# Rotary turns in a two-model kernel: halves exchanged by DMA in place of rotation products

## The reference

```python
def apply_rope(x, cos, sin):
    half = x.shape[-1] // 2
    xf = x.astype(jnp.float32)
    x1, x2 = xf[..., :half], xf[..., half:]
    return jnp.concatenate([x1 * cos - x2 * sin, x1 * sin + x2 * cos], axis=-1).astype(x.dtype)

qg = apply_rope(rms_norm(u_q.reshape(b, l, GQA_HEADS, HEAD_DIM), g_q_gqa), cos_g, sin_g)   # "a": 6 heads of 64, 2 key heads
qm = jnp.concatenate([qm[..., :64], apply_rope(qm[..., 64:], cos_m, sin_m)], axis=-1)      # "a": 6 MLA heads, last 32 of 96
q = rope(rmsnorm(two_map_heads(aq), q_norm_g), cos, sin)                                   # "b": 8 heads of 2 x 64, keys alike
```

## Time and profile before

| | us |
|---|---|
| median of 3 runs | 1923.73 (1923.69 to 1924.51) |
| profiled execution | 1922.46 |
| its span, first to last instruction | 1920.7 |
| PE busy | 1812.9 (94%) |
| DVE busy | 1103.0 (57%) |
| ACT busy | 886.3 (46%) |
| POOL busy | 378.6 (20%) |

### The profile page before, as it was taken

How to read it: one execution, slowest core, us unless ns; L and a number is a source line. 1 busy time by engine, 2 the same in 40 slices (tenths; PEclk the granted TensorE clock), 3 DMA queues, 4 the chain that set the end, 5 groups by cost and what they waited for, 6 DMA issues and landing times.

```text
span 1920.7 us, 28654 instructions
## 1 busy us (share of the span) xinstructions
PE 1812.9 (94%) x10864; PEld 1468.4 (76%) x10864; DVE 1103.0 (57%) x1955; ACT 886.3 (46%) x1773; POOL 378.6 (20%) x802
## 2 busy tenths in 40 slices
PE   4999999899999998988999989999999899999998
PEld 2453454588888885647999989888999797888998
DVE  3327841687777533482555567566556585664555
ACT  2227620433333333472555566565554464664542
POOL 1015100000000000240000025065451061364430
PEclk8799989999999999999899989999999999999999
DMA  8321631254555431302344533532344334332351
GB/s 303 104 86 54 216 126 44 88 175 176 176 175 187 163 88 40 117 1 78 142 176 176 176 132 105 187 116 101 135 160 176 128 104 176 132 132 88 133 177 65
DMA packets 139875, 255.26 MB, mean 133 GB/s; under 512 B 14926, under 2 KB 21724, under 8 KB 139612
## 3 DMA queue, kind: packets, MB, share of 16 engines
q1 hardware_dynamic: 138742, 251.16, 37.6%
q0 software_dynamic: 704, 2.10, 0.3%
q10 hardware_dynamic: 294, 0.18, 0.0%
HBM read 252.38 MB, written 1.05 MB: 132 GB/s over the span
## 4 chain that ended last, share of the span: by engine, by line
PE 83%; DVE 6%; ACT 4%; POOL 3%; issue 2%; SPq 1%; DMA 1%; ACTq 0%; DVEq 0%; POOLq 0%
PE ps L1127 17%; PE ps L1129 17%; PE ps L1128 17%; PE ps L1136 10%; PE ps L1021 3%; PE ps L1247 2%; PE ps L1273 1%; PE ps L1339 1%; PE ps L1341 1%; PE ps L1340 1%; PE ps L1259 1%; PE ps L1038 1%; PE ps L1101 1%; SPq L805 1%; PE ps L1419 1%
## 5 line engine op out<-in xcount | busy, mean ns | idle before, releaser
L1520 ACT ACTIVATE big_r<-ring 128x1024 fp32r<-128x1024 f32 x198 | 209.3, 1058 | 398.9 <-PE ps L1129 390.2
L1938 DVE TENSOR_TENSOR big_r<-ring,big_r 128x1024 fp32r<-128x1024 f32 x198 | 244.4, 1235 | 236.1 <-ACT big_r L1520 235.9
L1128 PE MATMUL ps<-big_r 128*128 128x256 f32 (+1 forms) x1120 | 373.7, 334 | 0.0
L1127 PE MATMUL ps<-hT_r,big_r 128*128 128x256 f32 (+1 forms) x896 | 291.8, 326 | 13.0 <-DVE big_r L1947 12.8
L1129 PE MATMUL ps<-hT_r,big_r 128*128 128x256 f32 (+1 forms) x896 | 284.5, 317 | 0.0
L1128 PEld LDWEIGHTS ps<-big_r 128*128 128x128 f32 x1120 | 215.2, 192 | 19.3
L1136 PE MATMUL ps<-hT,ring 128*128 128x512 f32 (+1 forms) x544 | 192.0, 512 | 10.9 <-ACT hT L1541 9.2
L1127 PE MATMUL ps<-big_r 128*128 128x256 f32 (+1 forms) x592 | 195.8, 331 | 1.4 <-DVE big_r L2095 1.4
L1127 PEld LDWEIGHTS ps<-hT_r,big_r 128*128 128x128 f32 x896 | 174.5, 195 | 29.0 <-issue 11.8
L1129 PE MATMUL ps<-big_r 128*128 128x256 f32 (+1 forms) x592 | 194.7, 329 | 0.0
L1129 PEld LDWEIGHTS ps<-hT_r,big_r 128*128 128x128 f32 x896 | 174.4, 195 | 10.3
(11 more groups left out here) (292 smaller groups left out, 4056.9 us busy)
## 6 DMA issues: line engine op xcount, KB each, us to landing
ring<-in_w_in SPq DMA_DIRECT2D x42, 2048.0 KB, 7.9
ring<-in_w_mlp SPq DMA_DIRECT2D x32, 2048.0 KB, 7.9
ring<-in_w_mod SPq DMA_DIRECT2D x24, 2048.0 KB, 8.0
ring<-in_w_out SPq DMA_DIRECT2D x4, 2048.0 KB, 8.0
ring<-in_w_out_a SPq DMA_DIRECT2D x4, 2048.0 KB, 7.9
ring<-in_w_out_b SPq DMA_DIRECT2D x4, 2048.0 KB, 8.2
ring<-in_w_o SPq DMA_DIRECT2D x4, 2048.0 KB, 7.9
ring<-in_w_in SPq DMA_DIRECT2D x12, 256.0 KB, 5.1
```

The lines of the kernel that those rows point to most:

```text
L1127: mm(b[:, 0:T], w_hi[:, k, :], hi(k), start=(k == 0), stop=False)
L1128: mm(b[:, 0:T], w_hi[:, k, :], lo(k), start=False, stop=False)
L1520: act_fn(hi, raw, ACT.Copy).then_inc(hi_ready, 1)
L1938: V.tensor_tensor(lo, raw, hi.bitcast(F32), ALU.subtract).then_inc(lo_ready, 1)
```

## The change

The rotation products are gone, with their constants, their entries in the plan of the PSUM banks and `ROT_LAG`. The units of a layer are put together in four *turns*: in "a" q0 and q1, then q2 and k, then the six qm, then the six km; in "b" four units each. For a turn POOL waits until all of its units are applied and then issues DMAs that write each half of their turned rows into the other half's place in a free buffer (`exchange`: four DMAs for 128 rows, two for the 32 rows of qm or km). When they have landed, POOL multiplies the whole turn by the cosine table in one instruction, DVE multiplies the exchanged halves by a sine table that now carries the sign, also in one instruction, and POOL adds the two (`turn`). For qm and km these three run over the 32 turned rows alone.

On POOL's queue the turns of "a" stand one after the other (exchange, turn, exchange, turn); in "b" the next turn's exchange is issued before a turn's cosine pass. On DVE's queue a sine pass stands several units behind the last unit of its turn (`SWAP_LAG`: 3, 4 and 6 in "a", 5 in "b"). The last one of "a" stands in the attention ahead of the maxima of step 3 (`SWAP_STEP`), the last two of "b" between the splits of av's granules. PE waits for a count of finished turns: before the attention of "a" for two, before its first MLA scores for all four, and before the first attention step of "b" for all four.

```diff
-ROT_LAG = 4
+SWAP_LAG = {"a": (3, 4, 6), "b": (5, 5)}
+SWAP_STEP = 3
...
-    put("rot64", P, rotation(P, [(0, 32), (64, 32)]))
-    put("rot96", MQK, rotation(MQK, [(MNOPE, MROPE // 2)]))
+    put("sign", P, np.where(np.arange(P) % HD < HD // 2, -1.0, 1.0)[:, None])
...
-    put("sing", P, np.tile(sg, (4, 1)))
+    put("sing", P, np.concatenate([-sg, sg, -sg, sg], 0))
...
+def turns_of(tag):
+
+    if tag[0] == "b":
+        return [[f"a{x}{c}" for c in range(n, n + 4)] for x in "qk" for n in (0, 4)]
+    return [["q0", "q1"], ["q2", "k"], [f"qm{h}" for h in range(MH)], [f"km{h}" for h in range(MH)]]
...
+        def turn_of(tag, t):
+
+            if tag[0] == "b":
+                units = (aqT, akT)[t // 2][:, 4 * (t % 2):4 * (t % 2) + 4, :]
+                return units, pT[:, t % 2, :, :], cos2[:, :], sin2[:, :], slice(0, P), HD // 2
+            if t < 2:
+                units = big[:, 0:4 * TOK].rearrange("p (c t) -> p c t", c=4)[:, 2 * t:2 * t + 2, LAT:]
+                return units, rs[:, :, :], cc("cosg"), cc("sing"), slice(0, P), HD // 2
+            units = (qmT, kmT)[t - 2][:, :, LAT:]
+            free = hT[:, 3:6, :].rearrange("p c (s t) -> p (c s) t", s=2)
+            return units, free, cc("cosm"), cc("sinm"), slice(MNOPE, MQK), MROPE // 2
...
-            def rope_units(tag, units, part):
...
-                    await_bank(pool, (tag, name, "rot"))
-                    link(nc.gpsimd.tensor_tensor(lat, lat, cos[0:parts, :], ALU.mult))
-
-                    await_drained(pool, (tag, name, "rot"))
-                    nc.gpsimd.tensor_tensor(lat, lat, rs[0:parts, n % 2, :], ALU.add).then_inc(roped, 1)
...
+            def exchange(tag, t):
+                units, free, _, _, rows, half = turn_of(tag, t)
+                for name in turns_of(tag)[t]:
+                    await_drained(pool, (tag, name, 0))
+                for o in range(rows.start, rows.stop, 2 * half):
+                    for to, of in ((o, o + half), (o + half, o)):
+                        pool.dma_start(free[to:to + half, :, :], units[of:of + half, :, :])\
+                            .then_inc(swap_landed[t % 2], 16)
+                        swaps[t % 2] += 16
+
+            def turn(tag, t):
+                units, free, cos, _, rows, half = turn_of(tag, t)
+                pool.wait_ge(swap_landed[t % 2], swaps[t % 2])
+                x = units[rows, :, :]
+                link(nc.gpsimd.tensor_tensor(x, x, cos[rows, :].unsqueeze(1).to_broadcast(list(x.shape)), ALU.mult))
+                pool.wait_ge(sine_made, turned(tag, t))
+                nc.gpsimd.tensor_tensor(x, x, free[rows, :, :], ALU.add).then_inc(roped, 1)
+                pool.wait_ge(roped, turned(tag, t))
...
-                rope_units(tag, units_a(i), 0)
-                rope_units(tag, units_m(i), 1)
+                for t in range(4):
+                    exchange(tag, t)
+                    turn(tag, t)
...
-                rope_units(tag, units_b(), 0)
+                exchange(tag, 0)
+                for t in range(4):
+                    if t < 3:
+                        exchange(tag, t + 1)
+                    turn(tag, t)
...
-                for j in range(n + ROT_LAG):
+                for j in range(n + max(MS_LAG, len(tail))):
...
-                    if 0 <= j - ROT_LAG and is_roped(units[j - ROT_LAG][0]):
-                        rotate(tag, units[j - ROT_LAG][0])
...
-                pe.wait_ge(roped, roped_before(tag, 1))
+                pe.wait_ge(roped, turned(tag, 1))
...
-                            pe.wait_ge(roped, roped_before(tag, 1) + 2 * MH)
+                            pe.wait_ge(roped, turned(tag, 3))
...
+                    if step == 0:
+                        pe.wait_ge(roped, turned(tag, 3))
...
+            def sine_product(tag, t):
+                _, free, _, sin, rows, half = turn_of(tag, t)
+                n_swaps[t % 2] += 16 * (rows.stop - rows.start) // half
+                dve.wait_ge(swap_landed[t % 2], n_swaps[t % 2])
+                x = free[rows, :, :]
+                V.tensor_tensor(x, x, sin[rows, :].unsqueeze(1).to_broadcast(list(x.shape)), ALU.mult)\
+                    .then_inc(sine_made, 1)
...
+                names = [name for name, _, _ in units]
+                at = {names.index(turn[-1]) + lag: t for t, (turn, lag) in enumerate(zip(turns_of(tag), SWAP_LAG[tag[0]]))}
...
-                    if len(pend) > 2 and pend[-3]:
-                        sine_product(tag, pend[-3])
+                    if j in at:
+                        sine_product(tag, at[j])
...
-                for name in pend[-2:]:
-                    if name:
-                        sine_product(tag, name)
+                    sine_product(tag, 2)
...
+                        if j == SWAP_STEP:
+                            sine_product(tag, 3)
...
                 run_units(tag, units_b())
+                lo_to(split_by((tag, "av", 1)))
+                sine_product(tag, 3)
                 lo_to(split_by((tag, "av", 3)))
```

87 lines of the change are left out of this document (22 added, 65 removed).

## The result

| | before | after |
|---|---|---|
| median of the runs | 1923.71 us (1920.39 to 1924.51) | 1942.17 us (1940.29 to 1944.23) |
| profiled execution | 1922.46 us | 1944.23 us |
| its span | 1920.7 us | 1942.4 us |

The change makes the kernel slower: the ratio of after to before is 1.0100, 95% interval 1.0082 to 1.0117. The forecast was 1911.7 us, so it is wrong by 30 us and on the wrong side.

What follows compares the result with a forecast made beforehand. PE was taken to bound the kernel, with 83% of the chain. Gains of 9.2 us ("b"), 1.2 and 1.3 (layers 0 and 1 of "a") and 0.3 (constants) sum to 12.0: median 1911.7 us, range 1903 to 1919.

Steps and rivals of the forecast that it cites:

- Rotations off PE in "b": Units of layers "b": 2 layers x 16 rotations x 0.43 us leave PE's chain, 13.8 us gross gain.
- Their replacement in "b": Longer POOL passes hold DVE and stall PE in "b": 2 x (0.8 + 1.5) us lost, net gain 9.2 us.
- The step from a hold to a stall: Turns 0 and 1 of "b": DVE 4.1 us late for one norm, PE stalled 0.4 us per turn (0 to 2).
- The end of the units: Sine passes 2 and 3 between av's splits in "b": the split PE needs comes 0 to 3 us late, 1.5 taken.
- rival (b): Every POOL pass holds DVE for its whole length; 3 to 6 us gained, 1918 to 1921; chance 0.13.
- rival (a): Collisions fit into PE's buffers, swaps land early, DVE gets its sine pass first; 20 us gained, 1903.5; chance 0.17.
- Layer 0 of "a": First maximum 4.2 us earlier, minus 3.0 us of DVE waiting and sine pass at step 3; net 1.2 gained (-1 to +3).
- Layer 1: In "a": first maximum 4.7 us earlier, minus 3.0 for sine 3 and 0.4 at MLA scores; net 1.3 gained (-2 to +3.5).
- Constants: Second load ahead of the first weights shrinks by 112 KB: 0 to 1 us gained, 0.3 taken.
- (c): Exchanges land late, DVE stands at sine 3 in "a" and "b"; slower by over 0.2% from about 9 us landing; chance 0.07.
- (d): The removed rotation products were covered, so nothing moves: 1923 us; chance 0.03.
- the signs by which the prediction said that it would be known as wrong: "b" period above 3.5 us, landings over 6 us, a later attention start, or layer 1 MLA-score wait over 2 us.

Runs made afterwards that it cites:

- the short passes: The kernel after with POOL's cosine passes and adds cut to 16 of each unit's 256 columns, turns incomplete; 1909.9 us, ratio to before 0.9935.
- the run with both edits: The kernel after with POOL's passes cut to 16 columns and the exchange filled from the cosine table, issued at a turn's first written unit; 1907.9 us.
- the run with km not turned: The kernel before without the km units' rotation products, sine products and POOL passes, nothing put in their place; 1923.0 us, ratio 1.0021.
- run with km kept warm: The kernel after with POOL's passes unit by unit, plus one unread PE product per km unit in "a"; 1919.6 us, ratio to before 0.9993.
- the fastest kernel: Against the kernel with only "b" changed: q0 to k exchanged too, POOL's passes unit by unit, qm and km still products; 1902.7 us, ratio to before 0.9922.

## Why the prediction was wrong

The profiled execution was forecast at 1910.5 us and took 1944.2. By the stages "b" is 18.4 us worse than forecast (9.2 lost instead of 9.2 gained), layer 0 of "a" about 7 and layer 1 9.4. One step failed in all three places, the price of a POOL pass that holds DVE; and in each of them PE's clock fell too, for which the sum has no term.

**Rotations off PE in "b"**, 13.8 us gross: right in kind. The period is 3.25 to 3.31 us. With POOL's long passes out of the way the two stages are 6.3 and 5.0 us shorter than before, 11.3 together, sine passes and exchanges included.

**Their replacement in "b"**, counted at 2.3 us per layer: this is the term that failed. It measured 10.7 and 9.8 us, the difference of the stages of after and of the short passes. Three things in its working were off.
- The step from a hold to a stall. The prediction saw the hold (sine held 1.6, then a Newton step held for most of the add, 4.1 us late) and its sizes came true: 2.5 and 1.7 us in turn 0, 2.5 and 1.7 in turn 1. Then it let PE's four banks swallow nearly all of it, 0.4 us left per turn (0 to 2). Turn 0 left 1.67. Turn 1's hold falls on ak5, and the product that waits for its bank is no unit but av's first granule, which fills two banks at once; there PE stands 5.05 us.
- What PE does after standing. The clock is at 0.51 between 1195 and 1200 us. The prediction has no term for that.
- The end of the units, taken at 1.5 us: the exchange of turn 3 landed after 7.4 us, and sine 3 and two splits were then held for 1 to 2.2 us each. With short passes the same landing costs nothing, as the run with both edits shows.

**Which rows to price it from.** The prediction took the price of a meeting from "a", 0.2 us paid by DVE. In "b", where the passes were to go, the rows of before say that POOL pays: 13 of its 16 adds took 1.6 to 1.7 us, and DVE's step 0.425 each time. That was the room which the change used up without a term in the sum. POOL's two passes of 0.74 and DVE's Newton step and split, 1.65 together, already made 3.1 of a unit's 3.73 us; POOL waited, off the chain, where a wait cost nothing. The change turned the waiting round.

The Trainium skill, "SBUF — State Buffer", section "Who interferes with whom", was weighed and half believed. The traces agree with it as to the full length of the hold (2.89 us of a Newton step for a POOL pass of 2.43), and rival (b), which took it at full price, was still too mild with 5 us per layer. The 9 us by which the prediction says that its sum would be better without the rule do not come out of its terms: the sum and rival (a), in which nothing is held, are 8 us apart. The same section says that DVE's `tensor_scalar` in its faster modes takes part in the exclusion though it has one input; the prediction left that out, and L2052 agrees, 2.94 us for a pass of about half a us while POOL's ran. The trace of before had it too: the same pass (L2056 there) took up to 1.31 us, beside POOL's pooling sums, where its median is 0.49.

**Layer 0 of "a"**: the last km unit at 178.14 (forecast 178.3) is right, its landing too: the halves are there 9.1 us after the last km unit (forecast 8.1 to 9.6). The upper end of that range is 0.5 us more than its terms give (1.75 + 3.7 + 1.1 + 2.5 = 9.05). The first maximum came 2.5 us sooner instead of 4.2, with PE at half clock ahead of it. Then DVE reached sine 3 not 8.4 but 12.6 us after the last km unit: a weights pass ahead of it was held for 2.1 us and PE's scores were slow. The attention took 8.2 us more than before where 3.0 were counted; some 3 us of such a difference can be the scatter of this stage.

**Layer 1**: 4.7 us sooner forecast, 0.6 us later measured. With the short passes it is 2.4 sooner; the missing 2.3 are close to the 1.8 us by which the first scores are slower in the run with km not turned, but that it is the same loss is not shown. The attention lost 7.5 us where 3.4 were counted. With short passes it loses 3.3: 1.75 for the sine pass, the rest beside a clock that falls once more at 841 us, so POOL's long passes in it were worth 4.2 us.

**Constants**, 0.3 us: too small to be read from any of the runs.

**The rivals.** (b) was the right mechanism and named the right place. Its price failed in the stall and the clock, by which it crossed to the slower side. (c) did not decide this run: the exchanges of "b" did land late, 6.7 us in the median, but with short passes that costs nothing, and those of qm and km landed in 2.3 us. The run with km kept warm shows its landing of over 7 us in the attention start. The prediction ruled it out by the idle DMA engines of the earlier trace rows; they are idle there in before, but SP's next weight load is issued in the same few us, and in the two traces shown the exchange lands in 2.4 us or in 7.2 by which of them comes first. (In "b" of after, too, it takes 6.4 to 7.4 us from the end of the issue while a weight load is under way or issued among its DMAs, and 2.4 to 2.7 where the load is nearly done.) (d) is out. Of the signs by which the prediction said that it would be known as wrong, two came: landings of over 6 us in "b", and an attention start of layer 1 that is later than before.

What stays open: why POOL's passes of 256 columns wait for DVE more often than those of 512 or 1024, where DVE waits; and where the 10 us of the fastest kernel come from that its stages do not show.

## What to carry to other kernels

Before work is merged into longer instructions on GpSimd, look at which of two engines waits for the other now, instance by instance (shortest, median and longest of a line), in the very stage that is to change: an engine that waits without harm is a reserve, and one long instruction can hand that wait to the engine on which everything hangs. Cutting POOL's passes back to one unit each was worth over 30 us here, more than the whole change was forecast to bring. And where an engine waits anyway, taking its work away buys nothing: leaving out PE's km products gained no time, and without them the clock of layer 1 fell ahead of the scores.

## What the runs showed of the hardware

- DVE can wait for the whole of POOL's pass even when its own record begins first: the Newton step at 1170.68 lies 0.17 us ahead of POOL's pass at 1170.85 and ended 0.29 us after it. The section of the Trainium skill named above has the one that issues first go first; by the starts in these records that does not always hold. With the same lead of 0.23 us the sine pass at 1186.64 was held by the cosine pass, and the split at 1175.14 held POOL's add (3.22 us instead of 2.4).
- POOL's passes that follow each other without a gap hold DVE as one: 3.01 us over two of 1.3, 3.29 us over four of 0.7.
- A `tensor_scalar` of 128x512 on DVE, 0.49 us alone, took 2.94 us beside a POOL pass.
- The same exchange of 96 KB landed 2.4 us after its issue or 7.2, by whether a 2 MB load had been issued just after it or just ahead of it.
- After 5.05 us in which PE stood, the granted clock was 0.51 (1.2 GHz) between 1195 and 1200 us. In the km stage of layer 1 it fell to that level (0.51 from 829 to 836 us) when the rotation products of 0.43 us, and the steps that hang on them, were left out.
